# Attention products of a head pair as 64-column products in two halves of the array, and flags of their own for the first loads of x

## The chip, the cores and the metric

The kernel runs on all 8 cores of one Trainium2 chip. Each core works alone on its own 2 of the 16 sequences; there is no exchange between cores. The metric is the device time of the slowest core in microseconds. Each core has TensorE (PE), which multiplies matrices into the eight banks of PSUM, VectorE (DVE), ScalarE (ACT), GpSimd (POOL), which here only issues the weight transfers, and SyncE (SP), which issues the transfers of x and of the results.

## The reference

One decoder layer over x of 16 x 2048 x 1024. A modulation computed from c (silu, one matrix, 6 x 1024 values per sequence) scales and shifts x into h. One projection of h gives q, k and v (12 heads of 64 in 3 groups), the input of a pooling mixer, and two gates.

- Attention: group g has dilation 1, 4 or 16, and each query sees itself and the 128 keys before it in its own residue class, with ALiBi. With p = exp(score + bias), a group gives a numerator sum(p v) and a denominator sum(p). The groups of one head slot are mixed by their denominators, which comes to (sum of the three numerators) / (sum of the three denominators). The result has 4 x 64 = 256 channels.
- Pooling: trailing means over 2, 4, 8 or 16 positions minus the token, a linear map per group, a scale.
- Both branches are projected to 1024, gated with sigmoids, added, and projected once more; then LayerNorm of alpha x + gate times that. Then a SwiGLU of width 2816 and a second LayerNorm in the same way.

## The kernel before

Everything is held transposed: channels on the 128 partitions, tokens along the free dimension. hT holds h for all 2048 tokens in bf16. Weights come in blocks of 8 x 256 columns (1 MB in memory, 512 KB as bf16) through a ring of NW = 6 slots. All requests for weights stand in one plan, in the order of use. pump() issues the next one on POOL's queue as soon as a slot is freed, which wfree() does after the last product that reads it. The engines keep in step by counters: a Reg remembers the last writer and the readers of a region, and an operation waits for these counts when they are not yet known to be reached.

**Start, sequence 0.** emit_consts0, then eight mod_unit (16 products of two tokens each, weights w_ada 4, 0, 5, 1, 6, 2, 7, 3: plan numbers 0 to 7). Number 8 is the first w_qk and number 9 the first w_v. After four of the units s0_first's load(tt, after) is called for the four x tiles of 512 tokens, with after = 3, 7, 8, 9: the transfer of the tile on SP waits for the weight of that plan number. The wait is taken from `r_w[ring["slot"][after]]` (line 448), the region of the ring slot that this weight was put in, as it stands when load is called. By then the four units have freed four slots, and numbers 6 to 9 have been issued into the slots of 0 to 3. mod(tt, m) turns a piece of x into hT, on ACT for even m and on DVE for odd m. Then the projections of phase 0 follow tile by tile: two qk units (512-token matmuls, line 369 in the helper mm_group) and two V units. SP next issues the tables, among them the bias of the scores.

**Attention.** Six phases (ph), each a group g and a head pair hp. att_phase has 8 + LAG = 10 slots. In slot i come the scores of block pair i (i < 8, line 591, keys 64 partitions high: head e_ = 0 in partitions 0 to 63, head 1 in 64 to 127), some fill units (the next phase's q and k projection; in sequence 0 also the other mod_units and the folding of pooling weights), and from slot 2 on out(i - 2) (line 636). Phases 1 and 3 have a V unit of the next group behind each out from the second on. In phase 5 the fill is the first pooling units with norm_units(0) among them. Scores go through DVE (line 605, adds the bias) and ACT (line 610, exp) into one of 2 x NPT = 12 slots for p in bf16.

V of a block lies in 384 columns of T3: v0, ones, v1, v2, ones, v3, with 64 columns each; line 1139 sets the ones by memset before phase 0. A product of out has 128 columns of this as weights: for even heads numerators land on output partitions 0 to 63 and denominators on 64 to 127, for odd heads the other way round. For each head of the pair and each of two blocks there is one product for the block itself and one for the block before, if there is one: 8, 6 or 4 in a call. One operation per call then copies (group 0) or adds (line 654) the bank into T1.

**Normalisation.** norm_units(hp) gives 8 units per head pair: logarithm and exp(-x) of the denominators on ACT (lines 668, 669, on 64 partitions x 1024), copies to the other half of the partitions through sg_t on DVE (673, 674), and the multiplications into attT (678, 680). norm_units(1) is spread one by one over the pooling units that follow phase 5 (seq_body, run with bg). In these, line 503 to 510 evict projections and band products, and line 747 corrects the first 16 tokens.

**Folding.** fold_units: fetch (transfer into sg_t), prep (line 772, eight DVE operations into ybs_t), and 16 units of products, in phases 1, 2 and 4 of sequence 0.

The rest (gates and output projection, LayerNorm, SwiGLU, lines 907 on) is not touched by the change.

## Time and profile before

| | |
|---|---|
| runs shown | 2041.25, 2259.1, 2422.63 us; median 2259.1 us |
| the profiled execution | 2041.4 us, its span 2040.4 us (cores 2037.0 to 2040.4) |
| PE busy | 1936.9 us, 11208 matmuls |
| DVE busy | 914.8 us |
| ACT busy | 795.5 us |
| mean granted PE clock, by core | 0.990 to 0.992 |
| moved by DMA | 193.42 MB, mean 95 GB/s |
| phases 0 to 5 | about 83 to 253 us, and 1077 to 1228 us |

The span runs from the first to the last instruction on the slowest core. PE's busy time is a union over overlapping matmuls; how long a matmul holds the engine is read from the distance between starts. The first number of a timeline row is the start and the second the length, both in microseconds; what stands in brackets is the idle time of the engine before it and what ended it. A clock of 1.00 is 2.4 GHz and 0.50 is 1.2 GHz; a mean between them says how the stretch was shared.

### The profile page before, as it was taken

How to read it: one execution, taken by the hardware profiler on the slowest of the kernel's cores; microseconds unless marked ns; L12 is line 12 of the kernel's file. 1: busy time of each engine (PE TensorE's matmuls, PEld its weight loads, DVE VectorE, ACT ScalarE, POOL GpSimd, SP SyncE). 2: the span in 40 equal slices, each digit the busy share in tenths (PEclk: the TensorE clock that was granted, in tenths of full speed). 3: DMA queues.
4: the chain of work that ended last, by engine and by line, in shares of the span. 5: the costliest groups of instructions: out<-in, count | busy, mean ns of one | idle time of the engine just before them, and what ended most of it. 6: DMA issues, size and time to landing. Idle time of an engine off the chain costs nothing.

```text
span 2040.4 us, 32395 instructions; the slowest of 8 cores (2037.0 to 2040.4 us)
## 1 busy us (share of the span) xinstructions
PE 1936.9 (95%) x11208; PEld 1005.4 (49%) x11208; DVE 914.8 (45%) x1434; ACT 795.5 (39%) x1343; POOL 141.3 (7%) x268
## 2 busy tenths in 40 slices
PE   0999999999999999999999998999999999999995
PEld 0566654444446644444455666444444564444442
DVE  0446653552325535534265666345331553542326
ACT  0555632551016326410266654246101642551026
POOL 1110100000000000000000000000000000000000
PEclk9999999999999999999999999999999999999998
DMA  8965734434435635456451123343543473434432
GB/s 161 245 107 96 147 100 87 64 67 77 83 73 106 185 63 106 80 120 150 82 114 42 32 53 104 74 73 64 91 79 66 103 183 77 73 63 73 82 63 83
DMA packets 58958, 193.42 MB, mean 95 GB/s; under 512 B 6832, under 2 KB 6832, under 8 KB 57520
## 3 DMA queue, kind: packets, MB, share of 16 engines
q0 software_dynamic: 38016, 136.20, 38.4%
q1 hardware_dynamic: 20784, 55.14, 8.1%
q8 instruction: 95, 1.56, 0.3%
q14 instruction: 63, 0.52, 0.1%
HBM read 300.24 MB, written 18.87 MB: 156 GB/s over the span
## 4 chain that ended last, share of the span: by engine, by line
PE 90%; DVE 4%; DMA 2%; issue 2%; ACT 1%; DVEq 0%; POOL 0%; ACTq 0%; SPq 0%; POOLq 0%
PE ps L369 80%; PE ps L1040 4%; PE ps L821 3%; PE ps L636 1%; PE ps L591 1%; DVE T L848 1%; DVE T L854 1%; DMA wring<-w_v 1%; DMA wring<-w_ada 1%; DMA T<-xT 1%; DVE T L605 0%; PE ps L411 0%; DVE u_t L508 0%; DVE T L654 0%; DVE attT L678 0%
## 5 line engine op out<-in xcount | busy, mean ns | idle before, releaser
L369 PE MATMUL ps<-T,wring 128*128 128x512 bf16 x4864 | 1078.5, 379 | 4.2 <-ACT sg_t L1001 4.2
L369 PEld LDWEIGHTS ps<-T,wring 128*128 128x128 bf16 x4864 | 475.7, 98 | 578.9 <-issue 6.7
L369 PE MATMUL ps<-hT,wring 128*128 128x512 bf16 x1792 | 416.0, 383 | 22.4 <-ACT hT L464 20.3
L1001 ACT ACTIVATE sg_t<-ps 128x512 f32<-128x512 f32 x176 | 103.2, 596 | 553.2 <-PE ps L369 546.4
L1002 DVE TENSOR_TENSOR T<-ps,sg_t 128x512 bf16<-128x512 f32 x176 | 120.3, 691 | 420.7 <-PE ps L369 379.6
L955 DVE SCALAR_TENSOR_TENSOR T<-ps,GA,T 128x512 f32<-128x512 f32 x256 | 192.1, 750 | 208.5 <-PE ps L369 205.9
L369 PEld LDWEIGHTS ps<-hT,wring 128*128 128x128 bf16 x1792 | 170.9, 99 | 228.9 <-issue 38.5
L369 PE MATMUL ps<-wring,hT 128*128 128x256 bf16 x1856 | 216.1, 275 | 5.5 <-ACT u_t L503 3.4
L369 PEld LDWEIGHTS ps<-wring,hT 128*128 128x128 bf16 x1856 | 186.1, 107 | 26.4 <-issue 7.2
L610 ACT ACTIVATE T<-T 128x256 bf16<-128x256 f32 (+1 forms) x232 | 104.3, 479 | 70.6 <-DVE T L605 64.1
L605 DVE TENSOR_TENSOR T<-ps,bias_t 128x256 f32<-128x256 f32 (+1 forms) x232 | 107.2, 499 | 52.0 <-PE ps L591 38.7
L809 ACT CAST ybs_t<-T 128x512 bf16<-128x512 f32 x128 | 79.0, 617 | 100.2 <-DVE T L955 100.0
L932 ACT ACTIVATE sg_t<-ps 128x512 f32<-128x512 f32 x64 | 38.2, 597 | 197.6 <-PE ps L369 197.5
L936 DVE TENSOR_TENSOR t_t<-ps,sg_t 128x512 f32<-128x512 f32 x64 | 44.3, 692 | 158.1 <-PE ps L369 158.1
L854 DVE TENSOR_TENSOR T<-T,st_t 128x512 f32<-128x512 f32 x128 | 87.5, 689 | 17.4 <-ACT st_t L841 11.0
L848 DVE TENSOR_TENSOR T<-T,st_t 128x512 f32<-128x512 f32 x128 | 87.1, 683 | 0.0
L1040 PE MATMUL ps<-T,wring 128*128 128x512 bf16 x384 | 84.8, 379 | 0.0
L654 DVE TENSOR_TENSOR T<-ps,T 128x512 f32<-128x512 f32 x64 | 69.9, 1092 | 28.3 <-PE ps L636 27.6
L810 ACT ACTIVATE ybs_t<-T 128x512 bf16<-128x512 f32 x128 | 80.2, 627 | 0.0
L821 PE MATMUL ps<-ybs_t,onesm 128*128 128x512 bf16 x256 | 75.3, 379 | 1.7 <-ACT ybs_t L809 1.4
L938 DVE TENSOR_TENSOR t_t<-ps,sg_t 128x512 f32<-128x512 f32 x64 | 44.3, 692 | 66.6 <-PE ps L369 66.6
L860 ACT ACTIVATE T<-T,B,G 128x512 bf16<-128x512 f32 x64 | 51.3, 813 | 36.4 <-DVE T L854 36.4
(81 smaller groups left out, 1064.2 us busy)
## 6 DMA issues: line engine op xcount, KB each, us to landing
wring<-w_gate POOLq DMA_DIRECT2D x44, 512.0 KB, 6.1
wring<-w_up POOLq DMA_DIRECT2D x44, 512.0 KB, 6.6
T<-xT SPq DMA_DIRECT2D x32, 512.0 KB, 7.8
wring<-w_down POOLq DMA_DIRECT2D x32, 512.0 KB, 6.9
outT<-T SPq DMA_DIRECT2D x64, 256.0 KB, 3.9
T<-xT SPq DMA_DIRECT2D x14, 1024.0 KB, 10.4
wring<-w_ada POOLq DMA_DIRECT2D x24, 512.0 KB, 8.9
wring<-w_pi POOLq DMA_DIRECT2D x16, 512.0 KB, 5.7
```

The lines of the kernel that those rows point to most:

```text
L369: fns = [lambda lhsT=lhsT, rhs=rhs, i=i: nc.tensor.matmul(psum[bank][:, cols[0]:cols[1]], lhsT, rhs, start=(i == 0), stop=(i == n - 1)) fo ...
L605: k.op(DVE, lambda tmp=tmp, src=src, bsrc=bsrc: nc.vector.tensor_tensor(tmp, src, bsrc, ALU.add), reads=[ps_reg[sbk[e_]], r_const], writes ...
L610: k.op(ACT, lambda pt=pt, tmp=tmp: nc.scalar.activation(pt, tmp, AF.Exp), reads=treg, writes=preg)
L809: k.op(ACT, lambda: nc.scalar.copy(ybs_t[:, i0, :], ysrc), reads=yreg, writes=[r_ybs[i0]])
L810: k.op(ACT, lambda: nc.scalar.activation(ybs_t[:, i0 + 1, :], ysrc, AF.Square), reads=yreg, writes=[r_ybs[i0 + 1]])
L821: k.group([lambda bk=bk, j=j: nc.tensor.matmul(psum[bk][:, :], onesm[:], ybs_t[:, i0 + j, :], start=(m == 0), stop=(m == KC - 1))], reads= ...
L848: k.op(DVE, lambda: nc.vector.tensor_tensor(yap, yap, st_t[:, 2 + 2 * tt, :], ALU.subtract), reads=yreg + [r_st[2 + 2 * tt]], writes=yreg)
L854: k.op(DVE, lambda: nc.vector.tensor_tensor(yap, yap, st_t[:, 1 + 2 * tt, :], ALU.mult), reads=yreg + [r_st[1 + 2 * tt]], writes=yreg)
L955: k.op(DVE, lambda: nc.vector.scalar_tensor_tensor(ydst, psum[bk][:, :], GA[:, gsel, m, b:b + 1], ydst, ALU.mult, ALU.add), reads=[ps_reg[ ...
L1001: k.op(ACT, lambda: nc.scalar.activation(sg_t[:, si, :], psum[bg][:, :], AF.Silu), reads=[ps_reg[bg]], writes=[r_sg[si]])
L1002: k.op(DVE, lambda: nc.vector.tensor_tensor(actT_ap(fl, tt * 512, 512), psum[bu][:, :], sg_t[:, si, :], ALU.mult), reads=[ps_reg[bu], r_sg ...
L1040: k.group([lambda bk=bk, sl=sl, fo=fo: nc.tensor.matmul(psum[bk][:, :], wv(sl, kk, fo, 128), h2ap(kk, tt), start=(kk == 0), stop=(kk == KC ...
```

## The change

Four things are changed.

- V is stored as 256 contiguous columns per block, without ones. The ones are a tile of their own, ones_t, of 64 columns. out makes numerators and denominators apart: for each block and key block, one product with 64 columns of V and one with ones_t, for each of the two heads, and the head e_ writes partitions 64 e_ to 64 e_ + 63 of the bank. Numerators of both heads lie in columns 0 to 255 and denominators in 256 to 511. There are 16, 12 or 8 products in a call. The two heads alternate.
- norm_units works on 128 partitions x 512 tokens, without copies: 4 x (logarithm, exponential; one multiplication).
- The flag of a weight's landing is kept per plan number (ring["landed"]), and load waits for that one.
- The memset of line 1139 is gone, the slots for p move in T3 and T4, and in the folds fetch stands first in phase 1 and prep last; phases 2 and 4 have 8 units each.

```diff
--- before.py
+++ after.py
@@ -232,6 +232,7 @@
         bands_t = k.sb("bands_t", [P, 12, 128], BF16)
         corr_t = k.sb("corr_t", [P, 4, 16], F32)
         onesm = k.sb("onesm", [P, P], BF16)
+        ones_t = k.sb("ones_t", [P, 64], BF16)
         cT_t = k.sb("cT_t", [P, KC, NB], F32)
         scT_t = k.sb("scT_t", [P, KC, NB], BF16)
         badaT_t = k.sb("badaT_t", [P, 48], F32)
@@ -327,7 +328,7 @@
         tl_pg = Tl(k.sem("dpg"))
 
         plan = []
-        ring = {"req": 0, "emitted": 0, "free": list(range(NW)), "slot": {}}
+        ring = {"req": 0, "emitted": 0, "free": list(range(NW)), "slot": {}, "landed": {}}
 
         def pump():
             if k.dry:
@@ -338,6 +339,8 @@
                 fn, rds = plan[j]
                 k.dma(POOL, tl_w[s], fn(s), reads=rds, writes=[r_w[s]])
                 ring["slot"][j] = s
+                ring["landed"][j] = Reg()
+                ring["landed"][j].w = r_w[s].w
                 ring["emitted"] += 1
 
         def wload(fn, rds=()):
@@ -392,6 +395,7 @@
             k.dma(SP, tl_c0, [(cT_t[:], cT), (badaT_t[:], b_adaT)], writes=[r_c0])
             k.op(ACT, lambda: nc.scalar.activation(scT_t[:], cT_t[:], AF.Silu), reads=[r_c0], writes=[r_sc])
             k.op(DVE, lambda: nc.vector.memset(onesm[:], 1.0 / D), writes=[r_ones])
+            k.op(DVE, lambda: nc.vector.memset(ones_t[:], 1.0), writes=[r_ones])
             k.op(DVE, lambda: nc.vector.memset(eps_t[:], LN_EPS / (ALPHA * ALPHA)), writes=[r_ones])
 
         def emit_consts1():
@@ -445,7 +449,7 @@
                 return t12_t[:, m - 4, :], [r_t12[m - 4]]
 
             def load(tt, after):
-                rds = [] if k.dry else [r_w[ring["slot"][after]]]
+                rds = [] if k.dry else [ring["landed"][after]]
                 src = xT[0].rearrange("(k p) t -> p k t", p=P)[:, :, tt * 512:(tt + 1) * 512]
                 regs = [r_ for m in range(KC) for r_ in stage(tt, m)[1]]
                 if tt < 2:
@@ -554,22 +558,21 @@
                         tts = sorted(set([ts.start // 512, (ts.stop - 1) // 512])) if g == 0 else range(4)
                         mm_group(bk, (j * 256, j * 256 + 256), [(hT[:, kk, ts], wv(sv, kk, 0, 256)) for kk in range(KC)],
                                  reads=[r_w[sv]] + [r_hT[kk][t_] for kk in range(KC) for t_ in tts], inc=(j == 1))
-                    copy_evac(eng or k.evac_eng(), aT3.A(gb * 384, [[192, 4], [128, 2], [1, 64]]),
-                              ps_ap(bk, 0, [[128, 4], [64, 2], [1, 64]]), None, [ps_reg[bk]], aT3.R(gb * 384, 768))
+                    copy_evac(eng or k.evac_eng(), aT3.A(gb * 256, [[1, 512]]), psum[bk][:, :], None, [ps_reg[bk]], aT3.R(gb * 256, 512))
                     if pr == 7:
                         wfree(sv)
                 units.append(u)
             return units
 
         def pt_ap(sidx, rel, dims):
-            if sidx < 4:
-                return aT3.A(6144 + sidx * 512 + rel, dims)
-            return t4b(4096 + (sidx - 4) * 512 + rel, dims)
+            if sidx < 8:
+                return aT3.A(4096 + sidx * 512 + rel, dims)
+            return t4b(4096 + (sidx - 8) * 512 + rel, dims)
 
         def pt_regs(sidx):
-            if sidx < 4:
-                return aT3.R(6144 + sidx * 512, 512)
-            return aT4.R(2048 + (sidx - 4) * 256, 256)
+            if sidx < 8:
+                return aT3.R(4096 + sidx * 512, 512)
+            return aT4.R(2048 + (sidx - 8) * 256, 256)
 
         def att_parts(ph):
             g, hp = divmod(ph, 2)
@@ -612,29 +615,22 @@
             def out(pr):
                 gb2 = 2 * pr
                 ob = new_bank()
-                fns, rds = [], []
-                for e_ in range(2):
-                    h = 2 * hp + e_
-                    vc = (0, 64, 192, 256)[h]
-                    scur = NPT * e_ + pr % NPT
-                    sprev = NPT * e_ + (pr - 1) % NPT
-                    for j in range(2):
-                        gb = gb2 + j
-                        n = gb % nb
-                        col = e_ * 256 + j * 128
-                        pairs = []
-                        if n > 0:
-                            if j == 0:
-                                pairs.append((aT3.A((gb - 1) * 384 + vc, [[1, 128]]), pt_ap(sprev, 256 + 128, [[1, 128]])))
-                                rds += pt_regs(sprev)
-                            else:
-                                pairs.append((aT3.A((gb - 1) * 384 + vc, [[1, 128]]), pt_ap(scur, 128, [[1, 128]])))
-                            rds += aT3.R((gb - 1) * 384, 384)
-                        pairs.append((aT3.A(gb * 384 + vc, [[1, 128]]), pt_ap(scur, j * 256, [[1, 128]])))
-                        rds += aT3.R(gb * 384, 384) + pt_regs(scur)
-                        for i, (lh, rh) in enumerate(pairs):
-                            fns.append(lambda lh=lh, rh=rh, i=i, col=col, n_=len(pairs): nc.tensor.matmul(
-                                psum[ob][:, col:col + 128], lh, rh, start=(i == 0), stop=(i == n_ - 1)))
+                fns, rds = [], [r_ones]
+
+                def acc(e_, col, lh, rh, first, final):
+                    fns.append(lambda: nc.tensor.matmul(psum[ob][64 * e_:64 * e_ + 64, col:col + 128], lh, rh, start=first, stop=final))
+                for j in range(2):
+                    gb = gb2 + j
+                    keys = [(gb, pr, j * 256)]
+                    if gb % nb > 0:
+                        keys.insert(0, (gb - 1, pr - 1, 384) if j == 0 else (gb - 1, pr, 128))
+                    for (kb, kp, rel) in keys:
+                        rds += aT3.R(kb * 256, 256) + pt_regs(kp % NPT) + pt_regs(NPT + kp % NPT)
+                    for den in range(2):
+                        for i, (kb, kp, rel) in enumerate(keys):
+                            for e_ in range(2):
+                                lh = ones_t[:] if den else aT3.A(kb * 256 + (2 * hp + e_) * 64, [[1, 64]])
+                                acc(e_, den * 256 + j * 128, lh, pt_ap(NPT * e_ + kp % NPT, rel, [[1, 128]]), i == 0, i == len(keys) - 1)
                 k.group(fns, reads=rds, writes=[ps_reg[ob]])
                 src = ps_ap(ob, 0, [[256, 2], [1, 256]])
                 o = 2 * hp * 2048
@@ -656,30 +652,18 @@
 
         def norm_units(hp):
             out = []
-            for hh in range(2):
-                c0 = hh * 1024
-                j0, j1 = 2 * hp, 2 * hp + 1
-                a0 = aT1.R(j0 * 2048 + c0, 1024)
-                a1 = aT1.R(j1 * 2048 + c0, 1024)
-                rr = r_sg[2 * hh:2 * hh + 2]
-                for (jj, p0_, ar) in ((j0, 64, a0), (j1, 0, a1)):
-                    def f(jj=jj, p0_=p0_, ar=ar, c0=c0):
-                        dv = aT1.A(jj * 2048 + c0, [[1, 1024]], p0_, 64)
-                        k.op(ACT, lambda: nc.scalar.activation(dv, dv, AF.Ln), reads=ar, writes=ar)
-                        k.op(ACT, lambda: nc.scalar.activation(dv, dv, AF.Exp, scale=-1.0), reads=ar, writes=ar)
-                    out.append(f)
-
-                def f2(c0=c0, a0=a0, a1=a1, rr=rr):
-                    k.op(DVE, lambda: nc.vector.tensor_copy(sg_ap(c0, 1024, 0, 64), aT1.A(j0 * 2048 + c0, [[1, 1024]], 64, 64)), reads=a0, writes=rr)
-                    k.op(DVE, lambda: nc.vector.tensor_copy(sg_ap(c0, 1024, 64, 64), aT1.A(j1 * 2048 + c0, [[1, 1024]], 0, 64)), reads=a1, writes=rr)
-
-                def f3(c0=c0, a0=a0, a1=a1, rr=rr, hh=hh):
-                    ra = r_attT[hp][2 * hh:2 * hh + 2]
-                    k.op(DVE, lambda: nc.vector.tensor_tensor(attT[0:64, hp, c0:c0 + 1024], aT1.A(j0 * 2048 + c0, [[1, 1024]], 0, 64), sg_ap(c0, 1024, 0, 64), ALU.mult),
-                         reads=a0 + rr, writes=ra)
-                    k.op(DVE, lambda: nc.vector.tensor_tensor(attT[64:128, hp, c0:c0 + 1024], aT1.A(j1 * 2048 + c0, [[1, 1024]], 64, 64), sg_ap(c0, 1024, 64, 64), ALU.mult),
-                         reads=a1 + rr, writes=ra)
-                out += [f2, f3]
+            for q in range(4):
+                no, do = hp * 4096 + q * 512, hp * 4096 + 2048 + q * 512
+
+                def f(do=do):
+                    dv, ar = aT1.A(do, [[1, 512]]), aT1.R(do, 512)
+                    k.op(ACT, lambda: nc.scalar.activation(dv, dv, AF.Ln), reads=ar, writes=ar)
+                    k.op(ACT, lambda: nc.scalar.activation(dv, dv, AF.Exp, scale=-1.0), reads=ar, writes=ar)
+
+                def f2(no=no, do=do, q=q):
+                    k.op(DVE, lambda: nc.vector.tensor_tensor(attT[:, hp, q * 512:(q + 1) * 512], aT1.A(no, [[1, 512]]), aT1.A(do, [[1, 512]]), ALU.mult),
+                         reads=aT1.R(no, 512) + aT1.R(do, 512), writes=[r_attT[hp][q]])
+                out += [f, f2]
             return out
 
         def att_phase(ph, fill, vroll):
@@ -1136,7 +1120,6 @@
                 run(qk_units(0) + v_units(0), bg, 1)
             while bg:
                 bg.pop(0)()
-            k.op(DVE, lambda: nc.vector.memset(aT3.A(64, [[384, 16], [192, 2], [1, 64]]), 1.0), writes=aT3.R(0, 6144))
             mods = [lambda it=it: mod_unit(it) for it in range(8, 24)] if b == 0 else []
             folds = fold_units() if b == 0 else []
             for ph in range(6):
@@ -1147,9 +1130,12 @@
                     nm = 3 if ph < 4 else 2
                     extra, mods = mods[:nm], mods[nm:]
                     if ph in (1, 2, 4):
-                        nf = {1: 1, 2: 9, 4: 8}[ph]
-                        extra += folds[:nf]
-                        folds = folds[nf:]
+                        if ph == 1:
+                            extra = folds[:1] + extra + folds[1:2]
+                            folds = folds[2:]
+                        else:
+                            extra += folds[:8]
+                            folds = folds[8:]
                     merged = []
                     for i, f in enumerate(fill):
                         merged.append(f)
```

## Rows read from the trace of the kernel before

**Rows 1.** The page: PE in the table of engines, and the chain by engine.

```profile
PE 1936.9 (95%) x11208; PEld 1005.4 (49%) x11208; DVE 914.8 (45%) x1434; ACT 795.5 (39%) x1343; POOL 141.3 (7%) x268
...
PE 90%; DVE 4%; DMA 2%; issue 2%; ACT 1%; DVEq 0%; POOL 0%; ACTq 0%; SPq 0%; POOLq 0%
```

**Rows 2.** Stretches after the last attention phase: PE's waits (total, times, longest), windows, timeline.

```profile
PE ps L369 <- DVE T L747: 4.1, 1, 4.1
PE ps L636 <- ACT u_t L503: 2.5, 1, 2.5
...
PE ps L369 <- DVE T L747: 5.5, 2, 4.1
...
228.00:290.00 62.00, 52.66 (x501) 40.96 (x498) 44.34 (x77) 33.57 (x53) 4.23 (x7) 0.92 0.57 145
1205.00:1262.00 57.00, 47.33 (x444) 37.52 (x443) 39.84 (x64) 32.18 (x50) 2.46 (x4) 0.91 0.42 116
...
261.78 1.84 PE L369 MATMUL ps<-bands_t,u_t 128*128 128x128 bf16 x30
...
277.49 3.36 PE L369 MATMUL ps<-bands_t,u_t 128*128 128x128 bf16 x30 [4.14 <-DVE T L747]
```

**Rows 3.** Start: chain of waits, timeline (start, length), a window (clock, DMA share last).

```profile
21.06 16.87 DMA wring<-w_v
...
38.43 10.68 DMA T<-xT
...
52.44 7.62 PE ps L369 x27
...
19.95 0.57 PE L411 MATMUL ps<-scT_t,wring 128*128 128x2 bf16 x16 [2.82 <-DMA wring<-w_ada]
...
31.59 0.57 PE L411 MATMUL ps<-scT_t,wring 128*128 128x2 bf16 x16 [2.20 <-DMA wring<-w_ada]
...
35.00:40.00 5.00, 0.00 (x0) 0.00 (x0) 0.00 (x0) 0.00 (x0) 0.00 (x0) 1.00 0.21 43
```

**Rows 4.** Groups by line and shape: xcount | busy us, mean ns | idle before.

```profile
L636 PE MATMUL ps<-T 128*128 128x128 bf16 x600 | 48.9, 220 | 4.4 <-ACT u_t L503 2.5 <-DVE T L654 1.4 <-DVE u_t L508 0.5
...
L636 PEld LDWEIGHTS ps<-T 128*128 128x128 bf16 x600 | 40.0, 98 | 18.3 <-issue 6.0
```

**Rows 5.** Timeline of PE, phases 0 and 1: start, length in us, what.

```profile
104.40 0.54 PE L411 MATMUL ps<-scT_t,wring 128*128 128x2 bf16 x16
104.81 0.61 PE L636 MATMUL ps<-T 128*128 128x128 bf16 x8
105.35 0.39 PE L591 MATMUL ps<-T 64*128 64x256 bf16 x4
105.67 3.63 PE L369 MATMUL ps<-hT,wring 128*128 128x512 bf16 x16
...
114.59 0.61 PE L636 MATMUL ps<-T 128*128 128x128 bf16 x8
115.04 1.91 PE L369 MATMUL ps<-wring,hT 128*128 128x256 bf16 x16
116.88 0.39 PE L591 MATMUL ps<-T 64*128 64x256 bf16 x4
```

**Rows 6.** Groups by line and shape, of the normalisation and like operations.

```profile
L941 DVE TENSOR_TENSOR T<-t_t 128x512 bf16<-128x512 f32 x64 | 44.3, 692 | 7.0 <-DVE t_t L938 0.5
...
L668 ACT ACTIVATE T<-T 64x1024 f32<-64x1024 f32 x16 | 16.9, 1053 | 6.6 <-DVE T L654 3.9 <-DVE A L427 2.4
...
L839 ACT ACTIVATE st_t<-st_t,eps_t 128x512 f32<-128x512 f32 x16 | 11.6, 723 | 9.3 <-DVE st_t L837 9.2
...
L678 DVE TENSOR_TENSOR attT<-T,sg_t 64x1024 bf16<-64x1024 f32 x8 | 9.7, 1214 | 0.0
...
L673 DVE COPY sg_t<-T 64x1024 f32<-64x1024 f32 x8 | 5.5, 690 | 2.6 <-ACT T L669 2.4
```

**Rows 7.** Timeline of PE, phase 2: the wait on the fold's preparation.

```profile
155.64 1.03 PE L369 MATMUL ps<-wring,ybs_t 128*128 128x256 bf16 x8 [3.61 <-DVE ybs_t L772]
```

## The prediction

> **What bounds the kernel now.** The header of the page comes first: TensorE (PE) is busy 95% of the span, and the chain that ended last is 90% PE [rows 1]. So an edit counts by what it does to the PE stream, or by what it removes from the few places where PE stands idle. The timeline of PE was read next, for the spacing of starts in the attention phases, because the busy figure of short matmuls overlaps itself. Then come the two stretches where the last attention phase and the pooling projections meet: PE idles 62.0 - 52.7 = 9.3 us in one and 57.0 - 47.3 = 9.7 us in the other, and the granted clock falls to 0.92 and 0.91 [rows 2]. The waits there name ScalarE (ACT) and VectorE (DVE) as what PE waited for [rows 2]. Last, the chain of waits from the start: PE has its first long run of matmuls at 52.4 us, and before it the chain is weight transfers and the transfer of x [rows 3].
>
> The sum is made against the profiled execution, 2041.4 us. That is 217.7 us below the median of the three runs shown and level with the lowest of them (2041.25), and the forecast is for that undisturbed level.
>
> **The attention products.** Today 600 products of 128 rows x 128 columns x 128 tokens make numerator and denominator together [rows 4]. Eight of them start 0.45 us before what follows (114.59 to 115.04 in [rows 5]), 56 ns each, 600 x 56 = 34 us. After the change there are 1200 products, each with 64 columns of weights (64 channels of V, or 64 ones), still with 128 moving tokens, alternating between output partitions 0 to 63 and 64 to 127. If the two of a pair run at once, a group of 16 takes the same 8 x 56 = 0.45 us, and the stream costs 0. If they run one after the other it costs 600 x 56 = +34 us. The trace shows no column halves. The nearest row is that of the scores, which use the array's row halves: four products of 256 tokens took 105.67 - 105.35 = 0.32 us [rows 5]. One after the other they would need 4 x 109 = 0.44 us (109 ns: the run of 16 after 115.04 gives way at 116.88, less the 0.09 named below); two pairs at once need 0.22, and 0.10 is left over. So halves do overlap there, and I take 0. The issue of 32 instructions for 8 slots of 56 ns fits too: 16 loads with 16 two-token products pass in 104.81 - 104.40 = 0.41 us [rows 5]. Below 0 there is nothing: each array half must still stream as many tokens as the whole did.
>
> **Changes of the array's division.** The 0.10 us left over has a partner on the way in: eight products followed by a full-width matmul take 0.45 us, the same eight followed by scores take 105.35 - 104.81 = 0.54 [rows 5]. Entering halves costs 0.09 and leaving them 0.10. The new product groups are in column halves, a third division. There are 8 groups x 6 phases x 2 sequences = 96. By the loop of att_phase, 50 are followed directly by scores (slots 2 to 6 of the phases without V units, the last slot before a new phase, and the first output of the phases with V units), and now pay one change more; 46 are followed by full-width work and pay two more. About 11 fewer are due where no fill unit stands before a group. That is about 131 changes x 0.10 = **+13 us**, all on PE. If row halves to column halves were free, 50 fall away: +8; the other end is that each costs double, +26.
>
> **Weight loads.** A load of 128 columns shows 98 ns in the trace and hides under products 56 ns apart [rows 4, 5]. If half the columns take half of that, 49 ns, and the loads of a pair cannot run side by side, a pair takes 98 ns instead of 56: 600 x 42 = +25 us. I take 0 and keep +25 as a case. The Trainium skill, page "TensorEngine Tiling (Array Packing)", section "Restrictions and Gotchas", says that column tiling shuts off the fast weight load, which speaks against this change; its page "TensorE: Matmul & The Clock Gate", section "LDWEIGHTS (loading the stationary operand)", gives columns / 1.2 ns, an estimate of 53 ns for 64 columns, and by it two unshared loads per pair would cost 600 x (107 - 56) = +31 us. No row before the change has a load in column halves, so the trace can't settle it.
>
> **Normalisation.** Numerators now fill partitions 0 to 127 in the order of the output. Per sequence and head pair, today: ACT runs 8 operations of 64x1024 at 1053 ns = 8.4 us; DVE runs 4 copies at 690 and 4 multiplications at 1214 = 7.6 us [rows 6]. After: ACT 8 operations of 128x512 at no more than the 723 of a logarithm of that shape = 5.8 us; DVE 4 multiplications at 692 (the nearest row of 128x512, f32 to bf16) = 2.8 us [rows 6]. That sheds 2.6 us of ACT and 4.8 us of DVE four times. Most of the time these engines are covered by PE, and the work is worth nothing. It is worth something where PE waits. The longest wait, 4.1 us at the end of the pooling units, occurs in both sequences; PE waits for evictions that queue on DVE behind the second head pair's copies and multiplications. The 2.5 us wait is for an eviction that stood on ACT behind the logarithms and exponentials of the first pair [rows 2]. I take those two kinds as gone, with most of the smaller ones. The clock goes with them: after the 4.1 us gap 30 products took 3.36 us which took 1.84 at full clock [rows 2], the step from 2.4 to 1.2 GHz. From the mean clock, half clock lasted 0.08 x 62 / 0.5 = 10 us and 0.09 x 57 / 0.5 = 10 us; part of it lies in the gaps, so some 4.5 us per sequence are lost. Idle 19 plus clock 9 is 28 at most; **-22 us**, with ends at -8 (the waits move to the next eviction) and -28. Late next is ACT's eviction of the last pooling units, by about half a microsecond each.
>
> **Loads of x.** The wait for the first x transfer looks up the ring slot of the fourth weight, but by then that slot holds the tenth (w_v), so the first x starts only when w_v has landed, at 37.9 us, and needs 10.7 us [rows 3]. The fourth weight's landing lets its products start at 19.95 [rows 3]. With the own flag x starts near 20. DMA is shared: from 20 us on five more weights (at some 3.2 us each, by the starts at 19.95 and 31.59 for four of them) and x (about 7 us of transfer) must land before the first projection, 20 + 16 + 7 = 43, instead of 52.4. The second x tile waits for the eighth weight, which now lands near 39 instead of 31.6; it lands near 51, and the projection for it stalls some 1.5 us. The queue of SP stands in order, so the later tiles and the tables follow, about 4 us earlier than today, since DMA was nearly idle (share 0.21) from 35 to 40 us [rows 3]. **-8 us**; ends 0 and -10. POOL's later weights wait on the last x tile and come 4 us earlier while PE wants them 8 us earlier; I count their margin as enough.
>
> **The rest.** The preparation of the folded weights moves from phase 2 to phase 1, which takes away the 3.6 us for which PE waited on it [rows 7]: **-3.6**; its eight short DVE operations lie beside products then. The two memsets of the ones in V go; they were DVE work ahead of the first bias addition of a sequence, under the projections that fill the slot: 0. V's evictions and those of the outputs keep their sizes: 0; the new memset of 64 columns lies in the idle start.
>
> Sum: 0 + 13 + 0 - 22 - 8 - 3.6 = -21, so 2041.4 - 20.6 = 2021, which I put at 2022 us, as the ends of the costs reach further up than down.
>
> **The rivals.**
> 1. Halves overlap, loads do not: +25 on the sum, 2046. For it: twice as many loads, each perhaps not cheaper; against it: the four loads of the scores, which run close together. 0.20.
> 2. The halves run one after the other: +34, 2055. For it: column halves share all 128 rows, and both need their own moving data; against it: the row halves. 0.16.
> 3. Slower by over 2%: loads neither shared nor hidden, so that each of the 1200 products takes 49 + 56 = 105 ns, +92 on the sum, 2113. Its place is the PE stream of the attention phases, 83 to 253 us and again in the second sequence. It decides against the change by over 2% from 62 us above my sum on, that is from 80 ns a product. For it: the third division of the array; against: loads hide now. 0.06.
> 4. Halves overlap, but the relief does not arrive (the norm waits move on, -8, and x gains nothing because the weights are held up as long as x is helped): 0 + 13 - 8 - 3.6, 2043. The change then doesn't do what its words say of the flags. 0.08.
>
> **How the numbers follow.** My case has 0.50 and its own range is 2008 (changes of division +8, normalisation -28, x -10, fold -3.6) to 2035 (the changes at twice the price, or the normalisation at -8). The range over cases goes from 2008 to 2062: it takes in rivals 1, 2 and 4 with 7 us above the second for a dearer change of division, and leaves out the third and the tails. A measurement of this kernel can tell about 2% (41 us) from no change. Faster by over 2% (below 2001) would need all ends at once and no price for switches: 0.03. Slower by over 2% (above 2082): rival 3 and a little, 0.07. Within: 0.90.
>
> **What would show it.** In the changed profile: 16 products of the output line in about 0.45 us (0.8 or more: rivals 1 and 2; 1.6: rival 3); 0.10 us before the first of them after a full-width matmul; first projection near 43 us; no PE wait over 1 us in the stretch after the last attention phase and a clock of 1.00 there; no wait on the fold. The prediction fails if the group takes much over 0.9 us, or if the earlier x leaves PE starved in the first 80 us.

## The result, and the profile after

The changed kernel's profiled execution took 2017.5 us where that of the kernel before took 2041.4. The ratio is 0.988, 95% interval 0.9863 to 0.9898: faster by 1.2%, within the 2% that was called no change, and beyond the measurement's own interval. A second run took 2017.53, and the forecast was 2022. The medians over all runs, 2150.39 us before and 2102.89 after, contain executions in which one die ran at a lower clock, as 2259.1 did; the comparison leaves those out, and the forecast has no term for them, so the second median lies outside its range of 2008 to 2062.

The page of the changed kernel: table of engines, and the chain by engine.

```profile
PE 1941.8 (96%) x11808; PEld 998.1 (50%) x11808; DVE 891.0 (44%) x1417; ACT 781.1 (39%) x1343; POOL 139.8 (7%) x268
...
PE 95%; DMA 2%; DVE 1%; ACT 1%; issue 1%; POOL 0%; DVEq 0%; ACTq 0%; SPq 0%; POOLq 0%
```

PE now carries 95% of the chain where it carried 90% [rows 1], although it has 600 matmuls more. The span is shorter because PE stands idle less, not because it has less to do.

The output products of the changed kernel, in the timeline of PE (start, length), one row of their weight loads from the same time, and the groups by line (x count | busy us, mean ns).

```profile
87.92 0.59 PE L372 MATMUL ps<-hT,wring 128*128 128x512 bf16 x2
88.45 0.30 PE L621 MATMUL ps<-T 128*64 128x128 bf16 x4
88.58 0.28 PE L621 MATMUL ps<-T,ones_t 128*64 128x128 bf16 x4
88.69 0.28 PE L621 MATMUL ps<-T 128*64 128x128 bf16 x4
88.81 0.28 PE L621 MATMUL ps<-T,ones_t 128*64 128x128 bf16 x4
89.02 0.39 PE L594 MATMUL ps<-T 64*128 64x256 bf16 x4
...
88.53 0.17 PEld L621 LDWEIGHTS ps<-T,ones_t 128*64 128x64 bf16 x4
...
L621 PE MATMUL ps<-T 128*64 128x128 bf16 x600 | 42.6, 226 | 0.0
L621 PE MATMUL ps<-T,ones_t 128*64 128x128 bf16 x600 | 41.4, 219 | 0.0
...
L621 PEld LDWEIGHTS ps<-T,ones_t 128*64 128x64 bf16 x600 | 27.7, 110 | 0.0
```

Sixteen products fill 89.02 - 88.45 = 0.57 us. Four of them start every 0.11 us, which is two pairs of 56 ns, so 8 x 56 = 0.45 is products and 0.12 the way out of the column halves; the way in takes 0.09 more (the first product of column halves comes 0.53 us after the first of two 512-token matmuls of 0.22 each). Before, eight products and the way into the scores took 0.54 together [rows 5]. A load of 64 columns shows 110 ns, not less than the 98 of a load of 128 [rows 4], and delays nothing. The loads of a pair run side by side: four of them pass in 0.17 us, which is one of 110 ns and a second pair 56 ns behind the first.

The two stretches from the first scores of a sequence to its first gate products, before and then after. In the kernel before, the second of them starts at 1071.03 us, not at the 1077 of the table of phases. The columns are the length, the busy time of PE, then of PEld, DVE, ACT and POOL; the clock stands third from last.

```profile
83.12:285.48 202.36, 189.23 (x1782) 129.31 (x1781) 125.33 (x228) 120.86 (x231) 17.59 (x32) 0.97 0.66 128
1071.03:1259.06 188.03, 175.30 (x1461) 115.63 (x1461) 122.00 (x203) 113.38 (x218) 6.70 (x12) 0.97 0.27 63
```

```profile
78.98:270.77 191.79, 191.79 (x2082) 125.99 (x2081) 113.52 (x219) 114.31 (x231) 16.89 (x32) 1.00 0.72 134
1056.32:1235.06 178.74, 177.88 (x1762) 111.77 (x1762) 110.17 (x194) 106.18 (x218) 6.34 (x12) 1.00 0.30 66
```

PE's waits in the changed kernel between 1040 and 1250 us (total, times, longest); between 78 and 270 us there are none:

```profile
PE ps L594 <- ACT T L507: 0.4, 1, 0.4
```

The stretches give the ledger. PE idled 13.1 and 12.7 us and now idles 0.0 and 0.9: -25.0, of which 19.0 are those of [rows 2] and 3.6 the fold's [rows 7]. PE's busy time rose by 2.6 in each: that is the price of the changes of division (entering or leaving row halves or column halves) less what the matmuls lost that ran at half clock and no longer do. With the first scores 4.1 us earlier, -25.0 + 5.2 - 4.1 = -23.9 of the 24.3 us that the span lost.

The start of the changed kernel: the chain of waits, then the transfers issued between 19 and 46 us (last number: median us from issue to landing).

```profile
19.62 25.58 DMA T<-xT
...
48.51 13.59 PE ps L372 x68
```

```profile
T<-xT SPq DMA_DIRECT2D x6, 1024.0 KB, 16.5
...
wring<-w_v POOLq DMA_DIRECT2D x1, 512.0 KB, 22.3
```

The first x is requested at 19.2 instead of 38.0, but takes 25.6 us where it took 10.7 [rows 3]. The first projection comes at 48.5, 3.9 us earlier. The products of the first modulation weights show when these landed:

```profile
19.25 0.56 PE L415 MATMUL ps<-scT_t,wring 128*128 128x2 bf16 x16 [1.82 <-DMA wring<-w_ada]
...
34.59 0.57 PE L415 MATMUL ps<-scT_t,wring 128*128 128x2 bf16 x16 [3.12 <-DMA wring<-w_ada]
```

Four more weights land in 15.3 us, 3.8 each, where it was 11.6 us, 2.9 each, without x beside them (19.95 to 31.59 in [rows 3]). The two queues between 25 and 30 us, q0 with the weights and q1 with x (packets, MB written, share of the 16 DMA engines):

```profile
q0 software_dynamic: 184, 0.66, 74.2%
q1 hardware_dynamic: 181, 0.37, 29.5%
```

### The profile page after: what moved, and what is told of

Its sections match the earlier page's. It is cut to its first block, busy times and chain, and to the rows that moved or that the text cites. A ratio compares the mean times of both kernels' runs of the same rounds, so it can differ in the third digit from the quotient of the medians.

```text
span 2016.1 us, 33562 instructions; the slowest of 8 cores (2013.8 to 2016.1 us)
## 1 busy us (share of the span) xinstructions
PE 1941.8 (96%) x11808; PEld 998.1 (50%) x11808; DVE 891.0 (44%) x1417; ACT 781.1 (39%) x1343; POOL 139.8 (7%) x268
## 4 chain that ended last, share of the span: by engine, by line
PE 95%; DMA 2%; DVE 1%; ACT 1%; issue 1%; POOL 0%; DVEq 0%; ACTq 0%; SPq 0%; POOLq 0%
PE ps L372 84%; PE ps L1024 4%; PE ps L805 3%; PE ps L621 2%; PE ps L594 1%; DMA T<-xT 1%; DMA wring<-w_ada 1%; DVE T L832 1%; DVE T L838 0%; PE ps L415 0%; DVE T L939 0%; ACT sg_t L985 0%; ACT u_t L507 0%; ACT hT L468 0%; POOL wring L189 0%
## 5 line engine op out<-in xcount | busy, mean ns | idle before, releaser
L507 ACT CAST T<-ps 128x512 bf16<-128x512 f32 x80 | 46.4, 580 | 53.7 <-PE ps L372 53.5
```

## Experiments

All were timed against the kernel before on the same chip. Two chips were used; the kernel before took 2040 to 2043 us on either. "Returned" means on top of the 2017.5 of the changed kernel, and is good to a microsecond or two.

### Own flags alone

```diff
...
-                rds = [] if k.dry else [r_w[ring["slot"][after]]]
+                rds = [] if k.dry else [ring["landed"][after]]
```

> The kernel before with one part of the change alone: each load of x waits for its own weight's flag. Theory A (the start gave 4 us, the first scores came at 79.0 instead of 83.1 us, and nothing later gives it back): 2037, first long run of matmuls near 48.5 us. Theory B (the earlier x is given back in the attention phases, because weights behind it come late): 2041, with waits of PE on weight transfers between 85 and 130 us.

Measured: 0.998 (0.997 to 0.9991), lowest 2036.7 us. The chain of waits at its start:

```profile
20.14 25.02 DMA T<-xT
...
48.48 11.56 PE ps L371 x55
```

The start is that of the changed kernel, 4.0 us earlier than before, and 3.5 to 4 us arrive at the end. Theory A holds.

### The two heads not in turn

```diff
-                for j in range(2):
+                for e2 in range(2):
+                  for j in range(2):
...
-                            for e_ in range(2):
+                            for e_ in (e2,):
```

> The changed kernel with the same 1200 products, but in a call all of head 0 first and then all of head 1, so that neighbours write the same half of the output partitions. Theory A (a pair runs at once only because its two products lie in different halves): 16 products take near 0.9 us instead of 0.45, 600 x 56 ns = +34 us, 2051. Theory B (64-column products are short by themselves, whichever half): no change, 2017.5. Theory C (the queue of PE looks ahead far enough to pair them all the same): also 2017.5, told from B by nothing here, but by starts in pairs 4 ns apart or not.

Measured: 0.9946 (0.9931 to 0.9961), 2030.6 us: 13 us returned. Timeline of PE:

```profile
88.01 0.30 PE L621 MATMUL ps<-T 128*64 128x128 bf16 x2
88.15 0.28 PE L621 MATMUL ps<-T,ones_t 128*64 128x128 bf16 x2
88.26 0.30 PE L621 MATMUL ps<-T 128*64 128x128 bf16 x4
88.37 0.31 PE L621 MATMUL ps<-T,ones_t 128*64 128x128 bf16 x4
88.51 0.28 PE L621 MATMUL ps<-T 128*64 128x128 bf16 x2
88.62 0.28 PE L621 MATMUL ps<-T,ones_t 128*64 128x128 bf16 x2
88.83 0.39 PE L594 MATMUL ps<-T 64*128 64x256 bf16 x4
```

At both ends products of one half come one by one, two in 0.11 us; in the middle four in 0.11. The group takes 0.82 us instead of 0.57. So Theory A is right that a product runs beside another only when that one is in the other half, but the time, 2030.6, lies far from both forecasts. The size was off: head 1's first products start while head 0's last are still due, which hides about four of head 1's eight, and calls of 12 and 8 products lose less (0.60 for 0.46, 0.36 for 0.35). 44 calls of 16 x 0.25 + 20 of 12 x 0.14 + 32 of 8 x 0.01 = 14 us, against 13 measured. The calls are counted from the loops (44 x 16 + 20 x 12 + 32 x 8 = 1200 products). The order in which the products are written is worth that much.

### The load of the old normalisation put back

```diff
                 def f2(no=no, do=do, q=q):
+                    k.op(ACT, lambda: nc.scalar.copy(t12_t[64:128, 0, :], aT1.A(no, [[1, 512]], 64, 64)), ...)
+                    for _ in range(2):
+                        k.op(DVE, lambda: nc.vector.tensor_copy(sg_ap(0, 1024, 0, 64), ...
```

> The changed kernel with work added to each of the normalisation units that the change had taken away, in size: two copies of 64x1024 on DVE (1.4 us) and one copy of 64x512 on ACT (0.6 us) in each of 4 units per head pair, with results that nobody uses. Before the change the difference was 4.8 us of DVE and 2.6 us of ACT per head pair. Theory A (the idle time of 22 us and the half clock after it vanished because these engines were relieved): most of it comes back, PE idle 6 to 10 us in each stretch after the last attention phase, a clock near 0.92 there, and 2037 to 2047. Theory B (what counts is the order and the smaller pieces, not the load): under 5 us come back, 2018 to 2022.

Measured: 0.9913 (0.9893 to 0.9933), lowest 2023.8 us: 6 us returned. The stretches of the last attention phase and the pooling units after it:

```profile
226.00:273.88 47.88, 44.33 (x475) 35.01 (x473) 39.39 (x77) 30.59 (x58) 2.15 (x5) 0.96 0.76 182
1206.00:1240.52 34.52, 32.64 (x362) 26.79 (x361) 30.50 (x56) 23.00 (x42) 1.58 (x3) 1.00 0.65 171
```

PE idles 3.6 and 1.9 us. Per head pair the added copies took 5.5 us of DVE and 2.5 of ACT. The change had taken away 4.9 of DVE and 3.4 of ACT (8.4 before, 5.0 after), more on ACT than the 2.6 that was forecast, so ACT got back only some 70%. Theory A falls all the same: about as much work as the change had taken away, on the same engines and in the same stretch, brings back a quarter. Theory B's 2018 to 2022 is just missed too.

### The old kernel with its normalisation spread

```diff
-                        if i < len(nu):
-                            fill.append(nu[i])
+                        lo, hi = len(nu) * i // len(body), len(nu) * (i + 1) // len(body)
+                        fill += nu[lo:hi]
...
-            run(pj[2] + bd[1] + pj[3] + bd[2] + bd[3], bg, 1)
+            for i, f in enumerate(pj[2] + bd[1] + pj[3] + bd[2] + bd[3]):
+                f()
+                if i % 2 == 0 and bg:
+                    bg.pop(0)()
```

> The kernel before, with nothing of the change but the normalisation units laid further apart: the 8 units of the first head pair over all 12 pooling units of phase 5 instead of the first 8, those of the second over 15 pooling units (every other one) instead of 8. The work is the same. Theory A (the load must go, or the waits only move on): PE idles as much as before, 2037 to 2042. Theory B (a backlog on DVE and ACT of a few us, which a pause between units lets run off): idle and half clock go down by more than half, 2020 to 2028.

Measured: 1.0033 (1.0019 to 1.0047), 2048.5 us, outside both ranges, on A's side and slower than the kernel before: PE idles 9.1 us in 230 to 290 and 11.6 in 1205 to 1265, and the clock in the first is lower still.

```profile
230.00:290.14 60.14, 51.05 (x502) 41.09 (x500) 42.62 (x72) 33.84 (x53) 4.22 (x8) 0.86 0.55 132
1205.00:1265.04 60.04, 48.43 (x471) 38.46 (x470) 39.87 (x62) 33.36 (x52) 2.64 (x5) 0.91 0.33 89
```

### Size of the pieces, both ways

The changed kernel with pieces of 1024, and the old one with pieces of 512 (line 657 on: `for q in range(4)`, 512 columns instead of 1024).

```diff
-            for q in range(4):
-                no, do = hp * 4096 + q * 512, hp * 4096 + 2048 + q * 512
+            for q in range(2):
+                no, do = hp * 4096 + q * 1024, hp * 4096 + 2048 + q * 1024
...
```

> The changed kernel with its normalisation in two pieces of 128x1024 per head pair instead of four of 128x512; the work in elements is the same, each burst on ACT is 2.1 us instead of 1.25 and on DVE 1.2 us instead of 0.7. Theory A (the size of a burst in front of the evictions makes PE wait, since the evictions into one u_t tile alternate between ACT and DVE and each waits for the other): waits of PE of 1 to 4 us return, 2020 to 2028. Theory B (the copies, and the chain copy behind exponential behind logarithm on 64 partitions, made them): no waits, 2017 to 2019.

> The kernel before with nothing of the change, but its normalisation cut in pieces of 512 tokens: 16 units per head pair, spread over phase 5 and over 16 of the 20 pooling units, ACT 16 operations of 64x512 (10 us per head pair where it was 8.4), DVE 8 copies and 8 multiplications of 64x512 (about 8.9 us where it was 7.6). There is more work than before, in smaller bursts (0.8 to 1.4 us instead of 1.4 to 2.4). Theory A (size of bursts): idle and half clock mostly go, 2018 to 2026. Theory B (amount of work, or the copies): 2038 to 2046.

Measured: large pieces in the changed kernel 0.989 (0.987 to 0.9909), 2017.8 to 2020.5 us, with 0.0 and 1.0 us of PE's idle time in the two stretches; small pieces in the old one 0.9993 (0.9982 to 1.0004), lowest 2039.3 us. The stretches of the old kernel with small pieces:

```profile
228.00:282.67 54.67, 46.98 (x505) 38.85 (x504) 43.59 (x85) 37.11 (x69) 4.22 (x8) 0.97 0.57 137
1205.00:1256.46 51.46, 43.31 (x422) 35.27 (x421) 39.24 (x73) 33.56 (x63) 2.15 (x4) 0.87 0.34 94
```

PE still idles 7.7 and 8.2 us. The size of a burst, the theory formed after the two experiments above, is borne out neither way. But it was not changed quite alone, and the work moved against it both times: large pieces took ACT 4.2 us per head pair instead of 5.0, small pieces 10.1 instead of 8.4, and DVE 8.8 instead of 7.6.

### The old shape put back

Load in small pieces gave 6 us, large pieces without the load 0 to 3. This kernel has both, and the waits of DVE for ACT, on the new products. Per head pair ACT works 8.4 us and DVE 7.6, as in the kernel before.

```diff
+                def g(no=no, q=q):
+                    for _ in range(2):
+                        k.op(ACT, lambda: nc.scalar.copy(t12_t[64:128, 0:2, :]..., aT1.A(no, [[1, 1024]], 64, 64)), ...)
+                def h(do=do, q=q):
+                    k.op(DVE, lambda: nc.vector.tensor_copy(sg_ap(q * 1024, 1024, 0, 64), ...
+                    k.op(DVE, lambda: nc.vector.tensor_copy(sg_ap(q * 1024, 1024, 64, 64), ...
...
+                    k.op(DVE, lambda: nc.vector.tensor_tensor(t12_t[0:64, 2:4, :]..., ALU.mult), ...)
-                out += [f, f2]
+                out += [f, g, h, f2]
```

> The changed kernel, but each half of a head pair's normalisation has again the four units of before with their lengths: 2.1 us of ACT, 2.1 us of ACT, two copies of 64x1024 on DVE that wait for both, then 2.4 us of multiplications on DVE (half of the added results are used by nobody). Large pieces alone gave back nothing and added load alone 6 us. Theory A (load, bursts and the wait of DVE for ACT act together; each alone is below what the slack of the stretch absorbs): 2033 to 2044, PE idle 7 to 10 us in each stretch and clock near 0.92. Theory B (the relief has another source, such as the order in which PE reaches these units or the missing memset): 2022 to 2026, as with the load alone.

Measured: 0.9996 (0.9986 to 1.0006), 2041.4 us: 24 us returned, the whole gain. PE's waits in the first stretch (total, times, longest), and the windows:

```profile
PE ps L372 <- ACT T L509: 3.9, 1, 3.9
PE ps L621 <- ACT u_t L507: 2.2, 1, 2.2
PE ps L372 <- DVE T L514: 1.0, 1, 1.0
PE ps L372 <- DVE T L741: 1.0, 1, 1.0
```

```profile
227.12:290.00 62.88, 54.01 (x552) 40.96 (x551) 44.13 (x78) 34.71 (x54) 4.30 (x7) 0.97 0.59 143
1206.00:1262.00 56.00, 46.73 (x475) 36.41 (x474) 38.99 (x64) 32.29 (x50) 2.87 (x4) 0.94 0.44 119
```

DVE waits here for ACT's copies (count | busy us, mean ns | idle before):

```profile
L669 DVE COPY sg_t<-T 64x1024 f32<-64x1024 f32 x8 | 5.5, 690 | 8.9 <-ACT t_t L665 8.6
```

PE's waits are where they were before, 3.9 us at the end of the pooling units and 2.2 in phase 5 [rows 2], and PE idles 8.9 and 9.3 us. Nothing else of the change was undone. So the relief comes from the normalisation. The work put back in small pieces gave a quarter of it, large pieces without the work little or nothing, and all three together, work, large pieces and the wait of DVE for ACT, the whole. The wait alone, and the work in large pieces without the wait, were not run, so it is not shown that all three are needed.

### x first, V units ahead

```diff
...
                 pairs = ((4, 0), (5, 1), (6, 2), (7, 3))
+                load(0, None)
...
-                for tt, after in enumerate((3, 7, 8, 9)):
+                for tt, after in ((1, 7), (2, 8), (3, 9)):
...
-                    out(o)
-                    if o >= 1 and vroll:
-                        vroll[o - 1]()
+                    if o >= 2 and vroll:
+                        vroll[o - 2]()
+                    out(o)
...
```

> The changed kernel with two edits. The first x tile is requested at the very start, ahead of all waits, and in phases 1 and 3 the V unit stands ahead of the output products (one slot later), so that these are followed directly by scores. First: x shares the DMA with the first weights instead of the later ones; the eight w_ada, w_qk and this tile are 11 MB at 3.3 us each, 4 + 36 = 40 us, and the first projection comes near 42 instead of 48.5 us: -6. If the tables or the next tiles become the bound, 0. Second: 26 or so changes of the array's division fewer, 26 x 0.1 = -2.8 us (0 if row halves from column halves cost as much as both steps). Together 2008 to 2010; without the first 2015.

Measured: 0.9865 (0.9848 to 0.9882), lowest 2013.7 us: 4 better than the changed kernel, where 8 to 9 were expected. Timeline of PE:

```profile
42.08 4.55 PE L372 MATMUL ps<-hT,wring 128*128 128x512 bf16 x15 [3.19 <-DMA wring<-w_qk]
46.47 3.66 PE L372 MATMUL ps<-wring,hT 128*128 128x256 bf16 x32
54.22 0.62 PE L372 MATMUL ps<-hT,wring 128*128 128x512 bf16 x2 [4.09 <-DVE T L512]
```

The first projection comes at 42.1 as forecast, and then PE waits 4.1 us in the second tile. The expectation had named this as what would make the gain 0. The second edit also brought less than the forecast 2.8: by the timelines of PE some 15 more calls are followed directly by scores, worth some 1.5 us at 0.10 each (an estimate).

### Staggered x

The same with `((1, 5), (2, 7), (3, 8))` for the three later tiles.

> As the kernel with the first x tile requested at once and the V units ahead, but the second, third and fourth tile wait for the weights with plan numbers 5, 7 and 8 instead of 7, 8 and 9. There the first projection came at 42.1 us, and PE then stood 4.1 us for the second tile, requested at 38.3 and landed at 51.0. Theory A (the request was late): the second tile lands near 46, the wait falls to 1 us or less, 2010 to 2012. Theory B (the DMA moves its bytes in any order at the same rate, so the weights come later by what x gains): 2013 to 2015, a wait on a weight instead.

Measured: 0.9859 (0.9838 to 0.988), lowest 2012.0 us. PE's waits before 85 us:

```profile
PE ps L372 <- DMA wring<-w_qk: 4.8, 2, 4.2
PE ps L372 <- DVE T L512: 2.5, 1, 2.5
```

On the slowest cores the wait in the second tile shrinks from 4.1 to 2.5 us while those on w_qk grow from 3.2 to 4.8; the medians over the eight cores go from 3.5 to 2.0 and from 3.2 to 4.0. That speaks for Theory B on the rate of the DMA. What is left over, 1 us or so, is not clear of the spread of the runs (2012.0 to 2015.0 us here, 2013.7 to 2014.1 without the stagger). The lowest time of the study is this kernel's, 1.4% under the one before, though its interval overlaps that of the changed kernel.

### Whole products without copies

Two kernels keep the products of 128 columns, and so pay for no column halves. They take the own flags and the order of the folds from the change and request the first x tile at once; the second staggers the later tiles too. Their normalisation still works on 64 partitions, but without copies, since the exponential writes into the other half of the partitions.

```diff
-                        k.op(ACT, lambda: nc.scalar.activation(dv, dv, AF.Exp, scale=-1.0), reads=ar, writes=ar)
+                        k.op(ACT, lambda: nc.scalar.activation(sg_ap(c0, 1024, 64 - p0_, 64), dv, AF.Exp, scale=-1.0), reads=ar, writes=rr)
...
-                def f2(c0=c0, a0=a0, a1=a1, rr=rr):
...
```

> A kernel that takes of the change all but the column halves: products of 128 columns as before, own flags and the first x tile ahead of all, the folds in the new order, and the normalisation in pieces of 512 with the exponential writing straight into the other half of the partitions (no copies). From 2017.5: 15 us of changes of the array's division less, 6 us earlier start, and whatever the larger normalisation costs (64 partitions at a time: ACT 10 us and DVE 5.5 us per head pair). Theory A (burst size decides): 1997 to 2004. Theory B (the amount or the 64-partition chain decides): 2012 to 2020.

> The kernel before with its products of 128 columns, with own flags, the staggered start, the new order of folds, and a normalisation in its old pieces of 1024 whose exponential writes into the other half of the partitions, so that the copies fall away: DVE 4.9 us per head pair where it was 7.6 and is 2.8 in the changed kernel, ACT 8.4. With small pieces this design gave 2021 with 15 us of PE waits left. Theory A (the load on DVE and ACT decides): 2012 to 2018. Theory B (the chain of both engines over 64 partitions keeps the waits): 2020 to 2026.

Measured: 0.9903 (0.9885 to 0.992) with pieces of 512 and 0.9898 (0.9883 to 0.9914) with pieces of 1024, 2021.2 and 2020.8 us at the lowest. Both have the earlier start (first projection at 41.3 and 41.8 us) and are still slower than the changed kernel. Theory B holds for the second kernel; the first misses both ranges, on B's side. PE's waits of the second kernel between 60 and 290 us:

```profile
PE ps L371 <- ACT u_t L505: 1.7, 2, 1.0
PE ps L638 <- DVE T L656: 1.7, 2, 1.1
PE ps L371 <- ACT T L507: 1.7, 1, 1.7
```

They stand 9 us behind the staggered kernel with column halves. So what the halves cost on PE, some 15 us, they more than give back by what ACT and DVE no longer do, against this design of whole products; how much of the 9 us is the V units put ahead was not separated.

## Why the prediction was right or wrong

**Products, 0: right.** 16 products take the time of 8 (0.45 us of the 0.57). The row halves of the scores [rows 5] were the right model. The +34 of rival 2 did not come even with the heads written one after the other, which cost 13.

**Changes of division, +13: right, a little low.** In 0.09, out 0.12, against 0.09 and 0.10 from the scores. With scores behind a call pays 0.12 more, with full-width work 0.22: 50 x 0.12 + 46 x 0.22, less 1 for calls without a fill unit ahead, is 15.

**Weight loads, 0: right.** A load of half the columns is no shorter (110 ns against 98), but the two of a pair share the time, and the products stay 56 ns apart. The rule of the Trainium skill, page "TensorEngine Tiling (Array Packing)", section "Restrictions and Gotchas", that column tiling shuts off the fast weight load, agrees with that row as far as a load has not become shorter with its columns. The +31 us that the Trainium skill's formula, page "TensorE: Matmul & The Clock Gate", section "LDWEIGHTS (loading the stationary operand)", gave for loads one after the other did not come; nor did its estimate of 53 ns for 64 columns, where the trace shows 110. Rivals 1 and 3 are out.

**Normalisation, -22: right in place, low in size, half right in cause.** Measured are 19.0 us of idle time and some 10 at half clock, 29 in all: PE's busy time rose by 5.2 where the changes of division alone make it rise by 15. Putting the old shape back cost 24; PE's idle time came back (18.2 us), but the clock fell only to 0.97 and 0.94 where it had been 0.92 and 0.91. The step had held back 6 us for waits that move on; none did. And it named the backlog of work on ACT and DVE as the cause, which put back in small pieces returned only 6.

**Loads of x, -8: wrong in size, -4.** The failing step is "20 + 16 + 7 = 43". It is 5.5 us short of the 48.5 measured, in two parts. 3.3 us are missing because it sets the landing of x, 43, against a first projection, 52.4: between the two ACT and DVE turn x into hT, 3.3 us before (49.1 to 52.4) and after (45.2 to 48.5). The other 2.2 us are the landing itself, 45.2. The step let only the five weights needed share the DMA with x, and read 3.2 us for each where its two starts give 2.9. In fact everything requested took its share: w_v, issued at 20.4 and 22.3 us on its way by its row, landed at 42.7 and was served before the second half of x (45.2), and the second tile, asked for at 34.6, took some as well. x asked for 18.8 us earlier landed only 3.9 us earlier. The stall of 1.5 us that it counted in the second tile did not come: the eighth weight landed at 34.6 us, not near 39, and after the first projection PE has no wait before 300 us.

**Fold, -3.6: right.** The wait is gone and none came in its place.

Sum as measured: 15 - 29 - 4.1 - 3.6 = -22, and 2.4 us of small waits in the attention phases (25.0 - 19.0 - 3.6) that the prediction did not count: -24. It forecast -20.6. The two wrong sizes, 7 too little for the normalisation and 4 too much for x, cancelled in part, and that the sum came within 4 us is luck to that extent. The mechanism of the likeliest case held, and so did "within 2%". Rival 4 is out as well: the idle time did go, and the earlier x did gain something.

## What to carry to other kernels

Small products in two halves of the array cost nothing in themselves if neighbours lie in different halves; count the changes between full width, row halves and column halves instead, at 0.1 us each, and gain on the engines that no longer have to move data between partitions. An idle stretch of the bounding engine need not have a single cause: the work put back in small pieces gave 6 of 24 us, large pieces alone 0 to 3, and only with the wait between the engines as well did the whole come back. A transfer asked for earlier shares the DMA with whatever else is outstanding, so count all that is requested before it lands, not only what the first consumer needs, and add the work between the landing and the first use.

## What the hardware showed that was not expected

- Written one half after the other, products of the second half still began before those of the first were done: 0.82 us for 16, where one by one they would take 0.57 + 0.45 = 1.02.
- A load of 64 columns in column halves shows 110 ns, longer than the 98 of a full one, and two of them pass in each 56 ns.
- The 2 MB of the first x tile took 25.6 us beside weights of 1 MB each that still landed every 3.8 us, where they took 10.7 and 2.9 without each other: the queue of x had the smaller share, 30% of the DMA engines' time against 74% between 25 and 30 us.
